# Moving each expert's second product and further rounds behind the next expert's first product

## The reference, cut to what matters

```python
def moe(x, r_w, r_b, w1, w3, w2):
    t = x.reshape(-1, D_MODEL)                      # 320 x 1024
    ...                                             # router: two experts per token, gates
    out = jnp.zeros(t.shape, jnp.float32)
    for e in range(N_EXPERTS):                      # 16
        h = jax.nn.silu(t @ w1[e]) * (t @ w3[e])    # w1, w3: 1024 x 512
        out = out + gates[:, e:e + 1] * (h @ w2[e]) # w2: 512 x 1024
    return out.astype(x.dtype).reshape(x.shape)
```

## Time and profile before

| | us |
|---|---|
| median of 3 runs (lowest, highest) | 1187.49 (1184.72, 1192.29) |
| the profiled execution | 1192.26 |
| its span on the core | 1190.6 |
| TensorE busy | 1006.8 (85%) |
| experts of layer 0, first up to last put | 223.5 to 518.2 |
| experts of layer 1, first up to last put | 879.5 to 1174.3 |

### The profile page before, as it was taken

How to read it: one execution, slowest core, us unless ns; L and a number is a source line. 1 busy time by engine, 2 the same in 40 slices (tenths; PEclk the granted TensorE clock), 3 DMA queues, 4 the chain that set the end, 5 groups by cost and what they waited for, 6 DMA issues and landing times.

```text
span 1190.6 us, 14515 instructions
## 1 busy us (share of the span) xinstructions
PE 1006.8 (85%) x4808; PEld 501.1 (42%) x4809; DVE 411.1 (35%) x902; ACT 174.5 (15%) x333; POOL 101.6 (9%) x190
## 2 busy tenths in 40 slices
PE   3989898999989999849989785589798899999993
PEld 3656445533323333326646543344563233333331
DVE  2545445232232323361134322211521432332336
ACT  1000223111001110111123222111211011111000
POOL 2050000100000000023000002200010000000000
PEclk9999997699989999979889897799769899999998
DMA  7584524998769999938030102219637469999981
GB/s 208 156 265 111 191 101 143 379 374 297 252 216 350 379 379 386 368 99 277 14 141 1 40 23 67 88 64 360 236 123 243 158 226 374 379 380 378 383 306 45
DMA packets 131447, 266.68 MB, mean 224 GB/s; under 512 B 7338, under 2 KB 39110, under 8 KB 131379
## 3 DMA queue, kind: packets, MB, share of 16 engines
q1 hardware_dynamic: 121184, 237.75, 56.5%
q10 hardware_dynamic: 4979, 16.15, 3.9%
q0 software_dynamic: 5232, 12.08, 3.8%
HBM read 259.52 MB, written 7.15 MB: 224 GB/s over the span
## 4 chain that ended last, share of the span: by engine, by line
PE 73%; DVE 11%; DMA 6%; issue 4%; SPq 3%; ACT 3%; ACTq 0%; DVEq 0%
PE bank L942 11%; PE bank L934 11%; PE wide L934 9%; PE bank L974 4%; PE bank L872 4%; PE bank L760 3%; PE wide L872 2%; PE bank L1041 2%; PE wide L760 2%; PE bank L1693 2%; DMA w<-in_e_w 2%; PE bank L776 2%; DMA w<-in_state_conv 2%; DMA dbuf<-in_a_w_pw 2%; PE bank L1594 2%
## 5 line engine op out<-in xcount | busy, mean ns | idle before, releaser
L942 PE MATMUL bank<-w,dbuf 128*64 128x512 f32 x512 | 135.5, 677 | 18.3 <-DVE dbuf L1352 17.0
L934 PE MATMUL bank<-w,dbuf 128*64 128x512 f32 x512 | 118.0, 611 | 4.5 <-issue 1.4
L934 PE MATMUL wide<-w,dbuf 128*64 128x512 f32 x512 | 113.4, 595 | 0.0
L1357 DVE COPY dbuf<-bank 64x512 f32<-64x512 f32 x64 | 44.1, 689 | 138.5 <-PE bank L942 138.0
L974 PE MATMUL bank<-dbuf,ukT 128*128 128x512 f32 (+1 forms) x144 | 79.3, 654 | 12.7 <-DVE dbuf L1367 5.9
L942 PEld LDWEIGHTS bank<-w,dbuf 128*64 128x64 f32 x512 | 45.2, 152 | 84.8 <-issue 84.5
L934 PEld LDWEIGHTS bank<-w,dbuf 128*64 128x64 f32 x512 | 41.7, 141 | 76.5 <-issue 74.7
L1693 PE MATMUL bank<-ident,w 128*128 128x128 f32 (+1 forms) x192 | 34.0, 335 | 34.8 <-DMA w<-in_cache_ckv 26.5
L934 PEld LDWEIGHTS wide<-w,dbuf 128*64 128x64 f32 x512 | 35.4, 137 | 65.0 <-issue 63.9
L529 POOL COPY idx_col<-idx 64x1 int32 (+1 forms) x30 | 5.3, 177 | 611.1 <-PE bank L921 421.1
L516 POOL DMA_DIRECT2D w<-in_cache_kpe x64 | 34.3, 536 | 267.4 <-PE bank L1748 164.4
(11 more groups left out here) (341 smaller groups left out, 1325.9 us busy)
## 6 DMA issues: line engine op xcount, KB each, us to landing
w<-in_e_w SPq DMA_DIRECT2D x90, 2048.0 KB, 16.2
dbuf<-in_a_w_pw SPq DMA_DIRECT2D x16, 512.0 KB, 5.8
w<-in_cache_ckv SPq DMA_DIRECT2D x64, 128.0 KB, 2.2
w<-u_rows SPq DMA_DIRECT2D x32, 142.0 KB, 2.9
dbuf<-in_a_w_pw ACTq DMA_DIRECT2D x1, 4096.0 KB, 17.1
dbuf<-in_e_w SPq DMA_DIRECT2D x2, 2048.0 KB
dbuf<-in_b_w_o SPq DMA_DIRECT2D x1, 4096.0 KB, 14.1
x_tok<-in_e_w SPq DMA_DIRECT2D x2, 1536.0 KB, 11.5
```

The lines of the kernel that those rows point to most:

```text
L934: last = nc.tensor.matmul(bank[n * C:(n + 1) * C], x[:, k], w[n][k], start=(k == 0), stop=(k == KD - 1))
L942: last = nc.tensor.matmul(bank[n * C:(n + 1) * C], h[:, k], w[k][:, n * 512:(n + 1) * 512], start=(k == 0), stop=(k == 3))
L1357: last = V.tensor_copy(y_pair[s * C:(s + 1) * C, h * 512:(h + 1) * 512], B[4 + s][h * C:(h + 1) * C, :])
```

## The change: down and further rounds one up later

TensorE now issues up(e+1) ahead of finish(e), in a new helper `finish` that takes the place of `expert`. Inside finish the transposition of the hidden rows comes first, then (even experts) the puts of the previous pair, then `turn`, now of expert e+2 in place of e+1, then the down. ScalarE, VectorE and GpSimd walk through their steps in the matching order: ScalarE does SiLU of expert e+1 ahead of the further rounds of e and waits for the previous gating product before it writes the one SiLU buffer; VectorE gates expert e+1 between the hidden copy and the output copy of expert e. TensorE waits for a pair's additions before it enters the further rounds of an even expert. SyncE's program is the same.

```diff
--- before.py
+++ after.py
@@ -550,13 +550,13 @@
 
             gather(1, 1, g0 + 1)
             pool.wait_ge(cnt_set, l + 1)
-            further(0)
             with pool.Fori(0, (E - 2) // 2) as it:
                 for s in range(2):
                     e = it * 2 + s
                     pool.wait_ge(xe_turned, e + (g0 + 1))
                     gather(e + 2, s, e + (g0 + 2))
-                    further(e + 1)
+                    further(e)
+            further(E - 2)
             further(E - 1)
 
         def act_program(act):
@@ -684,6 +684,8 @@
 
             def silu(g, s):
                 act.wait_ge(up_done, g + 1)
+                if not (isinstance(g, int) and g == 0):
+                    act.wait_ge(hid_done, g)
                 nc.scalar.activation(act_b, B[1 + s][0:C], ACT.Silu).then_inc(act_done, 1)
 
             def copy_hot(n):
@@ -706,20 +708,26 @@
                 with act.Else():
                     pass
 
+            def begin(e, s, pair, last=False):
+                silu(e + g0, s)
+                if not last:
+                    xe_copy(e + (g0 + 1), 1 - s)
+                if s == 1:
+                    copy_hot(pair + 8 * l)
+
             xe_copy(g0, 0)
-            with act.Fori(0, (E - 2) // 2) as it:
-                for s in range(2):
-                    e = it * 2 + s
-                    silu(e + g0, s)
-                    xe_copy(e + (g0 + 1), 1 - s)
-                    if s == 0:
-                        copy_hot(it + 8 * l)
-                    further(e, s)
-            silu(g0 + E - 2, 0)
-            xe_copy(g0 + E - 1, 1)
-            copy_hot(E // 2 - 1 + 8 * l)
+            begin(0, 0, 0)
+            begin(1, 1, 0)
+            further(0, 0)
+            with act.Fori(0, (E - 4) // 2) as it:
+                begin(it * 2 + 2, 0, it + 1)
+                further(it * 2 + 1, 1)
+                begin(it * 2 + 3, 1, it + 1)
+                further(it * 2 + 2, 0)
+            begin(E - 2, 0, E // 2 - 1)
+            further(E - 3, 1)
+            begin(E - 1, 1, E // 2 - 1, True)
             further(E - 2, 0)
-            silu(g0 + E - 1, 1)
             further(E - 1, 1)
             for i in range(3):
                 act_norm(act, 2 * l + 1, i)
@@ -1020,19 +1028,18 @@
 
             p0 = E // 2 * l
 
-            def expert(e, s, w, n13, n2, n_next, pair):
-
-                do_up(e + g0, s, w, n13)
-                if s == 0 and not (isinstance(e, int) and e == 0):
+            def finish(e, s, w, n2, pair, n_next=None):
+
+                do_hidden(e + g0, None if s == 0 else pair + (p0 + 1))
+                if s == 0 and not (isinstance(pair, int) and pair == 0):
                     put_rows(pair + (p0 - 1))
                 if n_next is not None:
-                    turn(e + (g0 + 1), 1 - s, n_next)
-                if isinstance(e, int) and e == 0:
-                    pe.wait_ge(cnt_set, l + 1)
-                do_hidden(e + g0, None if s == 0 else pair + (p0 + 1))
+                    turn(e + (g0 + 2), s, n_next)
                 do_down(e + g0, s, w, n2)
                 if s == 0:
                     turn_hot(pair + p0)
+                    if not (isinstance(pair, int) and pair + p0 == 0):
+                        pe.wait_ge(added, (pair + p0) * PUTS)
                 further(e, s, w)
 
             pe.wait_ge(r_onehot, 4 * l + HOT_FIRST)
@@ -1045,13 +1052,25 @@
             to_slots(B[3][0:C, 0:E * (CHUNKS - 1)], hot_rest,
                      lambda n, m: right_rest[0:m, n].rearrange("p q e -> p (q e)")).then_inc(r_product, 1)
             v = 16 * 7 * l
-            expert(0, 0, 0, 2 * n1 + 32, n1 + 16, n + 16, 0)
-            expert(1, 1, 1, 2 * n0 + 32, n0 + 16, v + 16, 0)
-            expert(2, 0, 2, 48 * (l + 1), 32 * (l + 1), n + 32, 1)
-            with pe.Fori(0, (E - 4) // 2) as it:
-                expert(it * 2 + 3, 1, 0, it * 32 + (2 * n1 + 64), it * 16 + (n1 + 32), it * 16 + (v + 32), it + 1)
-                expert(it * 2 + 4, 0, 1, it * 32 + (2 * n0 + 64), it * 16 + (n0 + 32), it * 16 + (n + 48), it + 2)
-            expert(E - 1, 1, 0, 2 * n1 + 256, n1 + 128, None, E // 2 - 1)
+            do_up(g0, 0, 0, 2 * n1 + 32)
+            turn(g0 + 1, 1, n + 16)
+            pe.wait_ge(cnt_set, l + 1)
+            do_up(g0 + 1, 1, 1, 2 * n0 + 32)
+            finish(0, 0, 0, n1 + 16, 0, v + 16)
+            do_up(g0 + 2, 0, 2, 48 * (l + 1))
+            finish(1, 1, 1, n0 + 16, 0, n + 32)
+            do_up(g0 + 3, 1, 0, 2 * n1 + 64)
+            finish(2, 0, 2, 32 * (l + 1), 1, v + 16 + 16)
+            with pe.Fori(0, (E - 6) // 2) as it:
+                do_up(it * 2 + (g0 + 4), 0, 1, it * 32 + (2 * n0 + 64))
+                finish(it * 2 + 3, 1, 0, it * 16 + (n1 + 32), it + 1, it * 16 + (n + 48))
+                do_up(it * 2 + (g0 + 5), 1, 0, it * 32 + (2 * n1 + 96))
+                finish(it * 2 + 4, 0, 1, it * 16 + (n0 + 32), it + 2, it * 16 + (v + 48))
+            do_up(g0 + E - 2, 0, 1, 2 * n0 + 224)
+            finish(E - 3, 1, 0, n1 + 112, E // 2 - 2, n + 128)
+            do_up(g0 + E - 1, 1, 0, 2 * n1 + 256)
+            finish(E - 2, 0, 1, n0 + 112, E // 2 - 1)
+            finish(E - 1, 1, 0, n1 + 128, E // 2 - 1)
             put_rows(p0 + E // 2 - 1)
 
 
@@ -1393,22 +1412,25 @@
                 with dve.Else():
                     pass
 
-            for s in range(2):
-                gate_hidden(g0 + s, s)
-                copy_hidden(g0 + s, s)
-                copy_y(g0 + s, s)
-                further(s)
+            gate_hidden(g0, 0)
+            copy_hidden(g0, 0)
+            gate_hidden(g0 + 1, 1)
+            copy_y(g0, 0)
+            further(0)
             with dve.Fori(0, (E - 2) // 2) as it:
-                for s in range(2):
-                    e = it * 2 + s + 2
-                    if s == 0:
-                        build_pair(e, it + (p0 + 1))
-                    gate_hidden(e + g0, s)
-                    if s == 0:
-                        add_rows(it + p0)
-                    copy_hidden(e + g0, s)
-                    copy_y(e + g0, s)
-                    further(e)
+                copy_hidden(it * 2 + (g0 + 1), 1)
+                gate_hidden(it * 2 + (g0 + 2), 0)
+                copy_y(it * 2 + (g0 + 1), 1)
+                further(it * 2 + 1)
+                build_pair(it * 2 + 2, it + (p0 + 1))
+                copy_hidden(it * 2 + (g0 + 2), 0)
+                gate_hidden(it * 2 + (g0 + 3), 1)
+                add_rows(it + p0)
+                copy_y(it * 2 + (g0 + 2), 0)
+                further(it * 2 + 2)
+            copy_hidden(g0 + E - 1, 1)
+            copy_y(g0 + E - 1, 1)
+            further(E - 1)
 
             n = p0 + E // 2 - 1
             for i, (t0, m) in enumerate(TILES):
```

## The result

| us | before | the change |
|---|---|---|
| median (lowest to highest) | 1188.99 (1184.72 to 1192.29), 4 runs | 1251.38 (1247.93 to 1253.54), 4 runs |
| span of the profiled execution | 1190.6 | 1251.9 |

The ratio is 1.0516, 95% interval 1.0487 to 1.0545: 62 us slower, where 36 were forecast and the range ended at 1243. The sign and the mechanism were right, the size was too small.

What follows compares the result with a forecast made beforehand. Nearly full DMA queues and a 93% busy TensorE bound the late experts, so load issue times decide. Layer 0 +6.3, layer 1 +13.8 and clock +15.9 sum to +36.0 on 1187.49: 1223.5 us, range 1198 to 1243.

Steps and rivals of the forecast that it cites:

- the range: Whole kernel: time between 1198 and 1243 us, around a forecast of 1223.5.
- TensorE's work, 29.7 a pair: TensorE, per pair of experts: two ups 14.0, odd finish 4.9, even finish 10.8, together 29.7 us.
- The chain of issues, 20.1: Loads ahead of odd ups: three transfers issued together after an even down take 20.1 us, against 12.5 of work.
- The pair, 37.3 and 39.1 with the clock: Pair of experts in the full stretches: 20.1 + 7.0 + 10.2 = 37.3 us, against 32.5 and 33.1 before.
- the clock term: Ups behind long waits run partly at 1.2 GHz: 1.8 us more each, nine waits, +15.9 us.
- my three rows: Three ups behind a stretch with gaps in the old trace: 8.55, 8.17 and 9.71 us in place of 7.04.
- Layer 0, up(7) at 346.0: Layer 0: up(7) starts at 346.0 instead of 366.20, with 1.2 us allowed for up(6) waiting on weights.
- The end of a layer, 29.3: Each layer, from up(15) to the last put's end: 29.3 us, against 20.4 before.
- forecast 13.5 and 22.8 with the clock: Added time of layers 0 and 1, clock loss included; without it +6.3 and +13.8 us.
- Rival B: DMA queue stays full, weights set the pace at 17.2 us an expert: -16.6 us, 1171, faster; chance 0.06.

Runs made afterwards that it cites:

- the cut change: The change with only the first quarter of w1 and w3 transferred from expert 3 on: 1142.39 us, ratio 0.9585.
- the cured version: The change with only SyncE's order altered, w1 and w3 of expert e+1 issued ahead of w2 of expert e: 1178.39 us, ratio 0.9905.

## Why the prediction was right in kind and too small

- **TensorE's work, 29.7 a pair**: right, 29.7 in the cut change.
- **The chain of issues, 20.1**: the right mechanism, a little small. From the issue behind an even down to the odd up it took 20.65 on the mean of nine, 20.0 to 21.2 and once 22.9 (1017.29 to 1040.16), where the queue still held the loads that the even up between them waited 3.4 us for. That is 5 us over the nine. Undoing the order of issues, or the place of the puts, moved the time as the chain says, and late issue alone made a loss of the same size in the old order.
- **The pair, 37.3 and 39.1 with the clock**: 39.9 and 40.3. The step that failed most is the size of the clock term, "1.8 more on the mean". The ten ups that waited longest for weights took 9.43 on the mean where 7.04 was the full-clock time, 2.4 more (8.42 to 10.07); and ten waited, not nine. 24 us in place of 15.9, the upper end that I had given. Why it is more than in my three rows stays open. Those stood at most 1.1 us right before, the ten 4.1 to 8.9; but among the ten the loss does not grow with the wait: 4.07 us cost 3.0, 7.72 cost 1.4. The up behind a further round is slow in both kernels (8.55 and 9.71 before, 9.72 and 8.41 after) and no part of the miss.
- **Layer 0, up(7) at 346.0**: it came at 351.6, 350.7 with the 0.9 by which this run started later. I let up(6) wait 0 to 2.4 and missed up(5), which stood 4.1 us for weights and ran 10.07:

```profile
285.14 3.65 PE L950 MATMUL bank<-w,dbuf 128*64 128x512 f32 x16 [0.19 <-DVE dbuf L1371]
292.86 10.07 PE L942 MATMUL wide<-w,dbuf 128*64 128x512 f32 x32 [4.07 <-DMA w<-in_e_w]
```

  Its w1 and w3 were issued from 266.12 on, 26.7 us before it, where two pieces on an empty queue take 13.7: the queue was still behind with the loads of expert 4. The sum treated it as empty or full and not as late.
- **The end of a layer, 29.3**: the last puts (below) end 34.4 after up(15) in both layers, 5.1 more. 2.8 of that is the clock of the up, 1.7 a down at half clock (5.35 for 3.65) and 0.6 a wait for ScalarE.

```profile
532.50 0.59 PE L929 MATMUL wide<-ident,dbuf 64*128 64x64 f32 x5 [0.62 <-ACT ukT L693]
533.77 5.35 PE L950 MATMUL bank<-w,dbuf 128*64 128x512 f32 x16 [0.68 <-DVE dbuf L1371]
...
544.23 1.98 PE L982 MATMUL bank<-dbuf,ukT 128*128 128x512 f32 x4 [0.43 <-DVE dbuf L1386]
...
1233.64 1.98 PE L982 MATMUL bank<-dbuf,ukT 128*128 128x512 f32 x4 [0.43 <-DVE dbuf L1386]
```

- **In total**, from first up to last put, layer 0 took 321.8 us against 294.7 of the earlier trace rows and layer 1 326.4 against 294.8: +27.1 and +31.6, forecast 13.5 and 22.8 with the clock. That is a miss of 13.6 and 8.8, and 2.6 more lie ahead of and between the expert stretches, which I had left unchanged. Of these 25 us 8 are the clock, 5 the chain of issues, 5 the ends of the layers without the clock of their ups, 3 the longer wait ahead of up(5) and 2.6 lie outside the experts; some 2 are left.
- **The range** took each bound alone. Here the four terms that were off, the chain, the clock, up(7) of layer 0 and the end, erred to the same side.
- **Rival B**, the full queue, was the wrong forecast for the change but 1171 came near the 1178 of the cured version.

## What to carry to other kernels

When work on one engine is put in another order, the buffers it frees come free in another order too; a queue that issues the refills in a fixed order must be changed with it, or its first unmet wait holds back transfers whose buffers are long free. Before valuing idle time on an engine that runs beside a full queue, work out the pace of the bytes: here 34.4 us a pair, more than the 32.5 to 33.1 that the kernel before took while it lived on weights landed ahead, so nearly nothing was left to win. The order of release made the change 1% faster than the kernel before; the same edit with the old order of issues made it 5% slower.

## What was not expected of the hardware

The size of the clock's share was not expected. The up behind a wait of 4 to 9 us lost 1.4 to 3.0 us to the lower clock, and the granted clock of those stretches fell from 0.97 and 0.96 to 0.89 and 0.88; the Trainium skill (TensorE: Matmul & The Clock Gate, HAM oscillation) has this pattern, and the trace agrees. Keeping the engine busy with unused products held the clock at 1.00 in layer 0 and 0.99 in layer 1, and all but one of the odd ups behind them at 7.0 to 7.1.
